# A two-layer hybrid kernel: three short products put between halves of a token unit

## The chip, the cores and the metric

The kernel runs on one core of a Trainium2 chip. The metric is the device time of one execution in microseconds (us); the median of three executions of the kernel before is 1004.25 us (999.66, 1004.25 and 1004.96). A fourth execution, the one that was profiled, took 1006.0 us. The five engines are called by the profile's names: PE (TensorE's matmuls), PEld (its weight loads), DVE (VectorE), ACT (ScalarE), POOL (GpSimd) and SP (SyncE, which here only issues DMAs).

## The reference, cut to what matters

256 tokens of width 1024 go through two layers. Each layer is a mixer, a residual with layernorm, a routed feed-forward stage with 16 experts, and again a residual with layernorm.

```python
for layer in range(2):
    mix = _mixer_ab(h, ...) if layer == 0 else _mixer_cd(h, ...)
    h = _layernorm(ALPHA * h + mix, ...)
    ffn = _moe(h, w_router, b_router, ...)
    h = _layernorm(ALPHA * h + ffn, ...)

# _mixer_ab: proj = h @ w_in; 4 retention heads (from q, k, v, gate rg) and 4 mLSTM heads (q, k, v, gate mo, mi, mf)
#   retention: scores = (q k^T) * decay;  y = scores @ v;  head norm;  * silu(rg)
#   mLSTM:     qk = (q k^T) * exp(d - m); num = qk @ v; den = qk.sum(-1); h = num / max(|den|, ..) * sigmoid(mo); norm
# _mixer_cd: 4 gated (GLA) heads and 16 SSD heads
#   GLA:       scores = q k^T weighted by exp of summed log_alpha; y = scores @ v; head norm; * silu(gr)
# _moe: probs = softmax(h @ w_router); 2 of 16 experts a token; y = sum of weighted (silu(h Wg) * (h Wu)) Wd
```

All is float32. The whole sequence is worked in two token tiles of 128 in place of the reference's chunks of 64.

## The kernel before, in words

**Units.** Weights stream in units of 2 MB (1024 x 512 of an input projection, 512 x 1024 of an output projection or of an expert) into `ring`, a buffer of six slots. SP issues the loads in program order, and waits before each for the matmul that read the slot's last unit (`freed`, waited for in `stream` and `stream_two`, L565). The mixer of layer 0 has units ab0 to ab11, that of layer 1 cd0 to cd11; each is followed by four output units (`weights_out`) and 48 expert units, six to a pair of experts.

**How a unit is multiplied.** `feature_unit` leaves features on the partitions (moving `hT`, 256 tokens wide). `token_unit` leaves tokens on the partitions: for each token tile t, it runs 8 matmuls over k, with `hT` as weights and a 512-wide moving unit, into one PSUM bank, so a unit has two halves, t = 0 and t = 1, in the two banks of a pair. Both call `mm` (L698); one such float32 matmul is two records in the trace, so a half of a token unit is 16 records. The unit's slot is free for the next load when the second half has ended. `token_unit` can be told which halves (`ts`) and which k (`ks`) to do; it claims its bank at k = 0 and signals at k = 7.

**PSUM.** There are eight banks. A table `plan`, filled by `job`, `single_job` and `pair_job` in the order of the program, says which bank a product uses and how often the bank was used before. `pair_job` takes the pairs (0, 1) and (2, 3) in turns; `single_job` takes the first bank of the next pair in the same turns; `job` names its banks. `claim` lets PE wait until the engine that reads a bank's last product has read it (`stored`), and `wait_ready` lets DVE or ACT wait for a product (`ready`).

**Order.** Each engine's order is written out by hand and is strict: an instruction that waits holds up all behind it on its engine.

- *Around the router's correction product.* PE does ab2 and ab3, then `gate_turns` (four small transposes into bank 0 and four small products into banks 2 and 3), then the product `fix`, then ab4 and ab5, then the retention scores `s_ret(0)` and `s_ret(1)`. `fix` is one product, a matrix of ones with 64 columns that DVE makes in `logit_weights` (L1907 to L1910, twice; its last instruction increments `fix_in`). DVE's order is: copy of the gate columns out of bank 0 (L1899), `logit_weights` twice, `scaled_router` (L1913), eight instructions that read the gate rows from their two banks (L1942), the copy of `fix` (L1951), then `p_ret(0)`, which waits for `s_ret(0)`. `fix` is needed by the router's correction only, after the first layer's mixer.
- *Around the fourth mLSTM head's scores.* PE does ab10, `y_ml(0)`, `y_ml(1)`, `s_ml(2)`, `s_ml(3)`, ab11, `y_ml(2)`, `y_ml(3)`, then the output units. `s_ml(hd)` is written to bank 4 for even heads and 5 for odd ones; a bank comes free when DVE's `y_ml(hd - 2)` has copied the row sums from it (L2042). DVE does all of `y_ml(0)`, then `y_ml(1)`, then `p_ml(2)` and `p_ml(3)` (the weighting of the scores, L1970), then `y_ml(2)` and `y_ml(3)`.
- *Around the fourth gated head's scores.* PE does cd4's second half, `s_gla(2)`, cd5's first half, `s_gla(3)`, `y_gla(2)`, cd5's second half, `y_gla(3)`, cd6, cd7, and then the turns of the gated heads' results (`y_turn(1, 0)`), which wait for DVE's `y_gla(3)`. `s_gla(3)` waits for `kscale`, that is for the end of DVE's `gla_head(3)` (last line L2389, eight instructions, each behind an exponential of ACT). `y_gla(hd)` needs DVE's `p_gla(hd)` (L1970). DVE's order: `gla_head(2)`, `y_gla(0)`, `y_gla(1)`, `p_gla(2)`, `gla_head(3)`, `p_gla(3)`, `y_gla(2)`, `y_gla(3)`.

Of the kernel before, what the change touches and what calls it, by code (L numbers as in the profile page):

```python
# [17 lines left out]
KC = D // P  # L18
# [84 lines left out]
def build(nc, a, out):  # L103
    with ExitStack() as ctx:
# [208 lines left out]
        def job(name, *banks):  # L313
            plan[name] = {b: uses[b] for b in banks}
            for b in banks:
                uses[b] += 1
# [4 lines left out]
        def pair_job(name):  # L321
            job(name, *((0, 1), (2, 3))[flip[0] % 2])
            flip[0] += 1

        def single_job(name):

            job(name, (0, 2)[flip[0] % 2])
            flip[0] += 1
# [41 lines left out]
            pair_job(f"ab{n}")  # L370
        single_job("gate_cols")
        pair_job("gate_rows")
        single_job("fix")
        for n in (4, 5):
            pair_job(f"ab{n}")
        for hd in range(2):
# [63 lines left out]
        def first_of(name):  # L440
            return min(plan[name])
# [4 lines left out]
        def wait_stored(eng, name, b):  # L446
            eng.wait_ge(stored[b], plan[name][b] + 1)

        def unit_no(layer, n):
            return layer * (LAYER_UNITS + MOE_UNITS) + n  # L450
# [240 lines left out]
        def _(pe):  # L691
            def claim(name, b):

                if plan[name][b]:
                    pe.wait_ge(stored[b], plan[name][b])

            def mm(o, l, r, start=True, stop=True):
                return nc.tensor.matmul(o, l, r, start=start, stop=stop)  # L698
# [21 lines left out]
            def unit_in(n):  # L720
                pe.wait_ge(ring_full[n % RING], landed(n))

            def rest_in(n):
                pe.wait_ge(ring_rest[n % RING], landed(n))
# [18 lines left out]
            def token_unit(name, n, ts=range(TB), ks=range(KC)):  # L743

                unit_in(n)
                w = ring[:, n % RING, :].rearrange("p (k n) -> p k n", k=KC)
                for t in ts:
                    b = list(plan[name])[t]
                    for k in ks:
                        if k == 0:  # L750
                            claim(name, b)
                        if t == 0 and k == KC // 2:
                            rest_in(n)
                        last = mm(bank[b][:, :], hT[:, k, t * P:(t + 1) * P], w[:, k, :], k == 0, k == KC - 1)
                        if k == KC - 1:
                            last.then_inc(ready[b], 1)
# [41 lines left out]
            def values(name, b, n_prob, v, start_cols=0, width=DV, n_heads=1, den=None, tell=True, slots=None):  # L798

                for t in range(TB):  # L800
                    for j in range(t + 1):
                        lhs = slots[:, t * P:(t + 1) * P] if j == 0 else slots[:, SEQ:SEQ + P]
                        last = mm(bank[b][:, t * DV + start_cols:t * DV + start_cols + width], lhs, v(j),
                                  j == 0, j == t)
                return last

            def score_group(b, kk, qq, parts, start=True, stop=True):
                for j in range(2):
                    last = mm(bank[b][:, j * SEQ:j * SEQ + SEQ - j * P], kk[parts, j * P:(j + 1) * P],
                              qq[parts, j * P:SEQ], start, stop)  # L810
                return last
# [48 lines left out]
            def gate_turns():  # L860
                b0 = first_of("gate_cols")
                claim("gate_cols", b0)
                pe.wait_ge(gate_ok, 1)
                for q, row in enumerate((2, 4)):
                    for t in range(TB):
                        last = nc.tensor.transpose(bank[b0][:, (q * TB + t) * 16:(q * TB + t) * 16 + HEADS],
                                                   gate_row[0:HEADS, row, t * P:(t + 1) * P],
                                                   consts[0:HEADS, C_ID:C_ID + HEADS])
                last.then_inc(ready[b0], 1)
                for q, b in enumerate(plan["gate_rows"]):  # L870
                    claim("gate_rows", b)
                    for hd in (2 * q, 2 * q + 1):

                        last = mm(bank[b][:, (hd % 2) * SEQ:(hd % 2 + 1) * SEQ],
                                  consts[0:HEADS, C_ID + hd:C_ID + hd + 1].to_broadcast([HEADS, P]),
                                  gate_row[0:HEADS, 3, :])
                    last.then_inc(ready[b], 1)

            gate_turns()
            b0 = first_of("fix")  # L880
            claim("fix", b0)
            pe.wait_ge(fix_in, 1)
            mm(bank[b0][:, 0:4 * EXPERTS], all_ones, route[:, 4:6, :, :].rearrange("p a t e -> p (a t e)")) \
                .then_inc(ready[b0], 1)
            for u in (4, 5):
                token_unit(f"ab{u}", unit_no(0, u))

            def s_ret(hd):
                b = first_of(f"s_ret{hd}")
# [21 lines left out]
            def s_ml(hd):  # L911
                b = first_of(f"s_ml{hd}")
                claim(f"s_ml{hd}", b)
                if hd == 0:
                    for u in (6, 7):
                        for bb in plan[f"ab{u}"]:
                            wait_stored(pe, f"ab{u}", bb)
                score_group(b, feat[:, 12 + hd, :], feat[:, 8 + hd, :], full).then_inc(ready[b], 1)

            def y_ml(hd):  # L920
                b, bd = first_of(f"y_ml{hd}"), first_of(f"s_ml{hd}")
                claim(f"y_ml{hd}", b)
                pe.wait_ge(prob_ready, hd + 1)
                if hd == 0:
                    for u in (8, 9):
                        for bb in plan[f"ab{u}"]:
                            wait_stored(pe, f"ab{u}", bb)
                slots = prob[:, hd % 2, :]

                for t in range(TB):  # L930
                    for j in range(t + 1):
                        mm(bank[bd][:, 400 + t:401 + t],
                           slots[:, t * P:(t + 1) * P] if j == 0 else slots[:, SEQ:SEQ + P], ones_col[:, :],
                           j == 0, j == t)
                values("", b, 0, lambda j: tok[:, 2, j, hd * DV:(hd + 1) * DV], slots=slots) \
                    .then_inc(ready[b], 1)
# [18 lines left out]
            y_ml(0)  # L955
            y_ml(1)
            s_ml(2)
            s_ml(3)
            token_unit("ab11", unit_no(0, 11))
            y_ml(2)  # L960
            y_ml(3)

# [387 lines left out]
            def s_gla(hd):  # L1350
                b = first_of(f"s_gla{hd}")
                claim(f"s_gla{hd}", b)
                pe.wait_ge(kscale, hd + 1)
                mm(bank[b][:, P:SEQ], k_far[:, hd % 2, :], dec[:, hd, SEQ:])
                for i in range(SEQ // GLA_BLOCK):
                    j, c = i // 4, i * GLA_BLOCK
                    last = mm(bank[b][:, j * P + c:j * P + c + GLA_BLOCK], k_blocks[:, i, :],
                              feat[:, hd, c:c + GLA_BLOCK])
                last.then_inc(ready[b], 1)

            def y_gla(hd):
                b = first_of(f"y_gla{hd}")
                claim(f"y_gla{hd}", b)
                wait_stored(pe, f"s_gla{hd}", first_of(f"s_gla{hd}"))
                if hd == 0:
                    for u in (2, 3):
                        for bb in plan[f"cd{u}"]:
                            wait_stored(pe, f"cd{u}", bb)
                values("", b, 0, lambda j: tok[:, 0, j, hd * DV:(hd + 1) * DV],
                       slots=prob[:, hd % 2, :]).then_inc(ready[b], 1)  # L1370
# [8 lines left out]
            token_unit("cd4", unit_no(1, 4), (1,))  # L1379
            s_gla(2)  # L1380
            token_unit("cd5", unit_no(1, 5), (0,))
            s_gla(3)
            y_gla(2)
            token_unit("cd5", unit_no(1, 5), (1,))
            y_gla(3)
            feature_unit("cd6", unit_no(1, 6), plain)
            feature_unit("cd7", unit_no(1, 7), plain)
# [1167 lines left out]
```

## Time and profile before

| | |
|---|---|
| three executions, median | 1004.25 us |
| the profiled execution | 1006.0 us, span of its instructions 1004.2 us |
| PE busy | 964.2 us (96% of the span), 3984 records |
| PEld busy | 514.2 us (51%) |
| DVE busy / ACT busy / POOL busy | 298.6 / 223.9 / 15.3 us |
| mean granted clock of TensorE | 0.990 of full speed |
| moved by DMA | 278.86 MB, mean 278 GB/s |
| longest chain | PE 79%, DMA 15%, DVE 3%, issue 1%, ACT 1% |

A stretch is given as from:to in us from the start of the span. "PEclk" is the share of the full clock that TensorE was granted in it: 1.00 is 2.4 GHz and 0.50 is 1.2 GHz. In a timeline, the bracket behind a row is the idle time of that engine just ahead of it and who ended it. Busy time on PE is modelled, so an end can lie some hundredths of a microsecond after the next start; the distance from one start to another is the safer measure.

### The profile page before, as it was taken

The numbers are of one execution on the slowest core, as the hardware profiler recorded it, in microseconds if no ns is written. First come the engines' busy times: TensorE is split into PE (matmuls) and PEld (weight loads), VectorE is DVE, ScalarE is ACT, GpSimd is POOL, SyncE is SP. The second block draws the span as 40 slices with busy tenths as digits, with TensorE's granted clock in tenths as the row PEclk, the third lists the DMA queues.
The fourth block names the chain that finished last, engine by engine and source line by source line (L and its number), as shares of the span: only waits on it lengthen the run. The fifth ranks groups of instructions, "written<-read, shape, count | busy, mean of one in ns | idle before, by whom it ended". The sixth has DMA issues, their size and how long they took to land.

```text
span 1004.2 us, 10005 instructions
## 1 busy us (share of the span) xinstructions
PE 964.2 (96%) x3984; PEld 514.2 (51%) x3984; DVE 298.6 (30%) x773; ACT 223.9 (22%) x466; POOL 15.3 (2%) x29
## 2 busy tenths in 40 slices
PE   8989999999999999989999999999999999999986
PEld 7644775554543355333385557888445433443322
DVE  4230162321431212120335433564316111131203
ACT  1120243211121112110202433431532121111101
POOL 2000000000000000000000000000000000000001
PEclk9999999999999999999999989999999999999999
DMA  8982334153789999999994423352655899999993
GB/s 275 333 317 88 134 118 149 61 210 125 270 342 404 422 422 412 397 420 421 396 388 157 156 85 118 134 210 79 241 224 211 324 399 421 420 422 420 419 418 148
DMA packets 65780, 278.86 MB, mean 278 GB/s; under 512 B 8852, under 2 KB 9216, under 8 KB 41920
## 3 DMA queue, kind: packets, MB, share of 16 engines
q1 hardware_dynamic: 63856, 271.60, 69.0%
q0 software_dynamic: 1872, 6.53, 1.9%
q8 instruction: 37, 0.61, 0.2%
q14 instruction: 15, 0.12, 0.0%
HBM read 277.04 MB, written 1.06 MB: 277 GB/s over the span
## 4 chain that ended last, share of the span: by engine, by line
PE 79%; DMA 15%; DVE 3%; issue 1%; ACT 1%; SPq 0%; DVEq 0%
PE bank L698 75%; DMA ring<-in_moe_w_up 14%; PE bank L1068 1%; DMA ring<-in_w_in_ab 1%; PE bank L1429 1%; PE bank L1073 1%; PE bank L794 1%; PE bank L975 0%; ACT feat L1497 0%; PE bank L1016 0%; DVE stat L2279 0%; ACT rstd L1497 0%; DVE hT L2286 0%; DVE h L2521 0%; DVE yT L2389 0%
## 5 line engine op out<-in xcount | busy, mean ns | idle before, releaser
L698 PE MATMUL bank<-ring,hT 128*64 128x512 f32 (+1 forms) x800 | 277.1, 604 | 11.6 <-DMA ring<-in_moe_w_up 5.4
L698 PE MATMUL bank<-ring,feat 128*64 128x512 f32 (+1 forms) x1152 | 228.5, 595 | 2.9 <-ACT feat L1497 2.7
L698 PEld LDWEIGHTS bank<-ring,hT 128*64 128x64 f32 (+1 forms) x800 | 108.5, 165 | 161.0 <-issue 153.3
L698 PE MATMUL bank<-hT,ring 128*128 128x256 f32 x768 | 168.4, 380 | 1.3 <-DMA ring<-in_w_in_ab 1.1
L698 PEld LDWEIGHTS bank<-hT,ring 128*128 128x128 f32 x768 | 145.8, 191 | 21.4 <-DMA ring<-in_w_in_ab 1.9
L1497 ACT ACTIVATE feat<-bank 32x512 f32<-32x512 f32 (+3 forms) x128 | 60.9, 494 | 388.2 <-PE bank L698 244.6
L698 PEld LDWEIGHTS bank<-ring,feat 128*64 128x64 f32 (+1 forms) x1152 | 74.1, 131 | 142.5 <-issue 131.1
L698 PE MATMUL bank<-ring,yT 128*128 128x512 f32 x256 | 112.8, 595 | 0.0
L2269 DVE COPY feat<-bank 32x512 f32<-32x512 f32 (+1 forms) x56 | 38.5, 687 | 145.7 <-PE bank L698 145.2
L698 PEld LDWEIGHTS bank<-ring,yT 128*128 128x128 f32 x256 | 47.8, 190 | 55.5 <-issue 54.6
L2259 DVE TENSOR_TENSOR feat<-feat,bank 128x512 f32<-128x512 f32 x16 | 11.0, 688 | 175.8 <-PE bank L698 175.8
L1497 ACT ACTIVATE tok<-bank 128x512 f32<-128x512 f32 x28 | 16.3, 593 | 124.7 <-PE bank L698 124.7
L698 PE MATMUL bank<-tok,h 128*128 128x256 f32 x128 | 37.7, 429 | 0.9 <-DVE tok L2146 0.9
L698 PEld LDWEIGHTS bank<-tok,h 128*128 128x128 f32 x128 | 32.5, 331 | 11.4 <-issue 11.1
L1497 ACT ACT_TABLE_LOAD x26 | 33.4, 1283 | 2.1 <-PE bank L698 1.7
L1068 PE MATMUL bank<-feat 128*128 128x512 f32 x64 | 30.9, 607 | 1.0 <-ACT feat L1497 1.0
L2009 DVE SCALAR_TENSOR_TENSOR feat<-bank,cols_cd,feat 128x255 f32<-128x255 f32 (+2 forms) x48 | 23.1, 481 | 25.7 <-ACT feat L1497 24.6
L1497 ACT ACTIVATE feat<-feat 128x256 f32<-128x256 f32 (+1 forms) x40 | 16.9, 445 | 35.8 <-DVE feat L2009 35.7
L1497 ACT ACTIVATE rstd<-mv,eps 128x2 f32<-128x2 f32 (+1 forms) x20 | 5.9, 295 | 75.2 <-DVE mv L2085 42.5
L698 PE MATMUL bank<-tok,hT 128*64 128x512 f32 x48 | 21.3, 592 | 0.0
L1520 ACT ACT_TABLE_LOAD x16 | 20.5, 1283 | 0.3
L1068 PEld LDWEIGHTS bank<-feat 128*128 128x128 f32 x64 | 10.9, 191 | 16.8 <-issue 12.5
(251 smaller groups left out, 568.7 us busy)
## 6 DMA issues: line engine op xcount, KB each, us to landing
ring<-in_moe_w_up SPq DMA_DIRECT2D x60, 1024.0 KB, 17.1
ring<-in_moe_w_gate SPq DMA_DIRECT2D x56, 1024.0 KB, 14.2
ring<-in_moe_w_down SPq DMA_DIRECT2D x56, 1024.0 KB, 12.1
ring<-in_w_in_ab SPq DMA_DIRECT2D x24, 1024.0 KB, 9.1
ring<-in_w_in_cd SPq DMA_DIRECT2D x24, 1024.0 KB, 13.5
ring<-in_w_out_ab SPq DMA_DIRECT2D x8, 1024.0 KB, 5.9
ring<-in_moe_w_down SPq DMA_DIRECT2D x16, 512.0 KB, 17.3
ring<-in_w_out_cd SPq DMA_DIRECT2D x8, 1024.0 KB, 6.0
```

The lines of the kernel that those rows point to most:

```text
L698: return nc.tensor.matmul(o, l, r, start=start, stop=stop)
L794: last = nc.tensor.transpose(bank[b][:, k * SEQ + t * P:k * SEQ + (t + 1) * P], src[:, t, c * P:(c + 1) * P], ident)
L1068: return nc.tensor.matmul(bank[4 + 2 * t + q][:, :], selw_t[:, t, :], ye[:, t, q * 512:(q + 1) * 512], start=start, stop=False, skip_group ...
L1073: last = nc.tensor.transpose(bank[0][:, c * P:(c + 1) * P], hid[:, c:FF:FF // P], ident)
L1429: last = nc.tensor.matmul(bank[b][e * SSD_HD:(e + 1) * SSD_HD, c * SEQ + j * P:(c + 1) * SEQ], xdt[:, j, hd * SSD_HD:(hd + 1) * SSD_HD], p ...
L1497: return nc.scalar.activation(o, i, f, **kw)
L1520: act.preload_act_table_set("natural_log_exp_and_others")
L2009: ins = V.scalar_tensor_tensor(out=o, in0=bank[b][:, (m % 2) * SEQ:(m % 2 + 1) * SEQ - back], scalar=cols[:, c:c + 1], in1=o, op0=ALU.mult ...
L2259: V.tensor_tensor(hid, sil, bank[3][:, :], ALU.mult) \
L2269: ins = V.tensor_copy(ye[r, t, 512:1024], bank[3][r, :])
```

## The change

`fix` moves from the turns of the pairs to bank 5 and from ahead of ab4 to between ab4's halves. `s_ml(3)` moves from ahead of ab11 to between its halves. `y_gla(2)` now comes right after cd5's first half, and `s_gla(3)` comes after the first four of the eight k of cd5's second half. Since `fix` takes no turn any more, all later `pair_job`s have the other pair: ab4 has banks 0 and 1 (it had 2 and 3), ab5 has 2 and 3, and so on through both layers up to cd11, which has 2 and 3 (it had 0 and 1). The orders of DVE, ACT, POOL and SP in the program are unchanged.

```diff
@@ -370,7 +370,7 @@
         single_job("gate_cols")
         pair_job("gate_rows")
-        single_job("fix")
+        job("fix", 5)
         for n in (4, 5):
             pair_job(f"ab{n}")
@@ -877,13 +877,14 @@
             gate_turns()
+            token_unit("ab4", unit_no(0, 4), (0,))
             b0 = first_of("fix")
             claim("fix", b0)
             pe.wait_ge(fix_in, 1)
             mm(bank[b0][:, 0:4 * EXPERTS], all_ones, route[:, 4:6, :, :].rearrange("p a t e -> p (a t e)")) \
                 .then_inc(ready[b0], 1)
-            for u in (4, 5):
-                token_unit(f"ab{u}", unit_no(0, u))
+            token_unit("ab4", unit_no(0, 4), (1,))
+            token_unit("ab5", unit_no(0, 5))
@@ -955,8 +956,9 @@
             s_ml(2)
+            token_unit("ab11", unit_no(0, 11), (0,))
             s_ml(3)
-            token_unit("ab11", unit_no(0, 11))
+            token_unit("ab11", unit_no(0, 11), (1,))
             y_ml(2)
             y_ml(3)
@@ -1379,9 +1381,10 @@
             s_gla(2)
             token_unit("cd5", unit_no(1, 5), (0,))
+            y_gla(2)
+            token_unit("cd5", unit_no(1, 5), (1,), range(KC // 2))
             s_gla(3)
-            y_gla(2)
-            token_unit("cd5", unit_no(1, 5), (1,))
+            token_unit("cd5", unit_no(1, 5), (1,), range(KC // 2, KC))
             y_gla(3)
```

## Rows read from the trace of the kernel before

**Rows 1.** Busy time by stretch (engines, PEclk, DMA share, GB/s): the two expert stages.

```profile
290.00:494.00 204.00, 196.38 (x915) 76.78 (x912) 36.16 (x91) 29.59 (x61) 0.00 (x0) 0.99 1.00 413
...
785.00:990.00 205.00, 195.81 (x908) 75.13 (x911) 36.13 (x92) 27.90 (x58) 1.05 (x2) 1.00 0.98 405
```

**Rows 2.** Waits of SP's DMA queue: total us, times, longest.

```profile
SPq L565 <- PE bank L698: 434.1, 74, 23.5
```

**Rows 3.** Waits of PE: total us, times, longest.

```profile
PE bank L698 <- DMA ring<-in_moe_w_up: 5.9, 10, 1.4
PE bank L698 <- issue: 3.8, 2, 2.1
...
PE bank L698 <- DVE yT L2389: 2.2, 1, 2.2
PE bank L698 <- DVE rec L2042: 1.9, 1, 1.9
...
PE bank L698 <- DVE route L1910: 1.4, 1, 1.4
...
PE bank L698 <- DVE feat L1942: 1.1, 1, 1.1
```

**Rows 4.** Timeline of PE: gate rows, `fix`, ab4 with ab5; then ab8 with ab9.

```profile
68.76 1.97 PE L698 MATMUL bank<-spare,consts 4*128 4x256 f32 x8
72.16 0.41 PE L698 MATMUL bank<-route,consts 128*128 128x64 f32 x2 [1.43 <-DVE route L1910]
73.67 30.75 PE L698 MATMUL bank<-ring,hT 128*128 128x512 f32 x64 [1.10 <-DVE feat L1942]
...
142.40 27.63 PE L698 MATMUL bank<-ring,hT 128*128 128x512 f32 x64
```

**Rows 5.** Timeline of DVE beside it: gate columns' copy, gate rows' readers.

```profile
68.93 0.18 DVE L1899 COPY gate_col<-bank 128x16 f32<-128x16 f32 x1 [14.50 <-PE bank L866]
...
72.13 2.69 DVE L1942 SCALAR_TENSOR_TENSOR feat<-bank,gate_col,consts 128x256 f32<-128x256 f32 x8
```

**Rows 6.** Busy time and clock by 2 us, in ab4's first half.

```profile
74.00:76.00 2.00, 2.00 (x3) 0.80 (x3) 0.95 (x4) 0.00 (x0) 0.00 (x0) 0.50 0.85 313
```

**Rows 7.** Timeline of PE: `s_ml(2)`, `s_ml(3)`, ab11.

```profile
190.59 0.82 PE L698 MATMUL bank<-feat 128*128 128x256 f32 x4
193.27 0.92 PE L698 MATMUL bank<-feat 128*128 128x256 f32 x4 [1.86 <-DVE rec L2042]
194.03 13.90 PE L698 MATMUL bank<-ring,hT 128*128 128x512 f32 x32
```

**Rows 8.** Timeline of PE: cd4's second half to cd7.

```profile
576.87 7.03 PE L698 MATMUL bank<-ring,hT 128*128 128x512 f32 x16
...
583.74 0.38 PE L698 MATMUL bank<-yT 128*128 128x128 f32 x2
...
585.66 7.11 PE L698 MATMUL bank<-ring,hT 128*128 128x512 f32 x16
595.03 0.60 PE L698 MATMUL bank<-yT 128*128 128x128 f32 x2 [2.25 <-DVE yT L2389]
...
608.59 1.46 PE L698 MATMUL bank<-tok,spare 128*128 128x256 f32 x6
609.88 27.79 PE L698 MATMUL bank<-hT,ring 128*128 128x256 f32 x128
```

**Rows 9.** Timeline of DVE beside it: `p_gla(2)`, end of `gla_head(3)`, last of `y_gla(3)`.

```profile
590.31 0.55 DVE L1970 SCALAR_TENSOR_TENSOR spare<-bank,consts 128x384 f32<-128x384 f32 x1
...
592.92 1.96 DVE L2389 SCALAR_TENSOR_TENSOR yT<-yT,feat 128x128 f32<-128x128 f32 x8
...
614.36 0.88 DVE L2416 SCALAR_TENSOR_TENSOR tok<-bank,rstd,tok 128x256 f32<-128x256 f32 x2 [0.60 <-ACT rstd L1497]
```

**Rows 10.** Busy time and clock by stretch: `s_gla(3)`; then 440:450.

```profile
596.00:600.00 4.00, 4.00 (x17) 3.82 (x17) 0.56 (x1) 0.46 (x1) 0.00 (x0) 0.50 0.02 4
...
440.00:450.00 10.00, 9.03 (x35) 3.53 (x37) 3.39 (x11) 0.21 (x1) 0.00 (x0) 0.83 1.01 419
```

## The prediction

> **What bounds the kernel now.** I read the page first: PE is busy 96% of the span and is 79% of the chain that ended last. So any time in which PE stands idle, or runs at the lower clock, outside a stage that something else sets, is time of the kernel. I then asked for busy time by stretch, to find stages with another limit. The two expert stages are such: the DMA engines are busy for 1.00 and 0.98 of them at 413 and 405 GB/s, with PE busy for 196.38 of 204 us and 195.81 of 205 [rows 1]. Everything that the change touches lies in the mixers, ahead of these stages.
>
> The third question is whether time won ahead of an expert stage is kept behind it. The waits of SP's queue answer it: in the expert loads SP stood 434.1 us, in 74 waits, for a matmul to free a slot [rows 2]. The loads do not run by a clock of their own. They start when PE has finished with the slots, so an earlier PE makes them start earlier, and the same number of bytes then ends earlier by as much.
>
> The fourth view is the list of PE's waits. Four rows in it belong to the change: 1.4 us for DVE's `logit_weights` (L1910), 1.1 for the gate rows' readers (L1942), 1.9 for the row sums of `y_ml(1)` (L2042) and 2.2 for `gla_head(3)` (L2389) [rows 3]. They sum to 6.6 us. The last view is the timeline around each with the granted clock, and it shows a second cost: behind two of the three places PE runs at clock 0.50, which is 1.2 GHz [rows 6, 10].
>
> **The change part by part.** I take each place from a start ahead of it to one behind it, and rebuild the same list of work at the pace that the trace has for it undisturbed.
>
> *`fix` between ab4's halves.* Now: the gate rows end at 68.76 + 1.97 = 70.73; PE waits 1.43 us, runs `fix` in 0.41, waits 1.10, and ab4 with ab5 end at 73.67 + 30.75 = 104.42. That is 33.69 us [rows 4]. The two units took 30.75 us where ab8 with ab9, the same 64 records, took 27.63 [rows 4]; the 3.12 us between them are the lower clock, 0.50 in 74:76 [rows 6]. After: ab4's first half can start at 70.73. Its bank is now 0, which DVE had emptied at 68.93 + 0.18 = 69.11 [rows 5]. A half lasts 27.63 / 4 = 6.9 us, so `fix` comes up at 77.6; its input was there by 72.16, when it ran before [rows 4]. Bank 5 was last used by the gate products, long read. ab5 now has banks 2 and 3, which hold the gate rows until 72.13 + 2.69 = 74.82 [rows 5], and it claims them at about 85. New stretch: 27.63 + 0.41 = 28.04. Gain 33.69 - 28.04 = 5.65 us, of it 2.53 idle and 3.12 clock. On DVE the copy of `fix` now waits until 78; behind it stands `p_ret(0)`, which waits for a score product that PE makes after ab5, at 98.8, so nobody feels it. Bank 5 goes next to `s_ret(1)`, 20 us later. The idle time is hidden by ab4's first half; if bank 0 were not free, the wait would be back at the same place.
>
> *`s_ml(3)` between ab11's halves.* Now, from the start of `s_ml(2)` to that of ab11: 194.03 - 190.59 = 3.44 us, with a wait of 1.86 us in it. One undisturbed score product is 194.03 - 193.27 = 0.76, two are 1.52 [rows 7]. Gain 1.92 us. Here the idle time brought no lower clock: ab11's 32 records took 13.90 us [rows 7], and half of ab8 with ab9 is 13.8 [rows 4]. After, `s_ml(3)` comes up at 191.35 + 6.9 = 198.3 on the old scale; its bank was read by 193.27, when it ran before [rows 7]. Nobody is late next: DVE's `p_ml(3)` follows in half a us and `y_ml(2)` and `y_ml(3)` stand behind another 6.9 us half. ACT's work on ab11's first half comes earlier, not later.
>
> *`y_gla(2)` ahead, `s_gla(3)` between the quarters.* Now, from the start of cd5's first half to that of cd6: 609.88 - 585.66 = 24.22 us [rows 8]. Undisturbed prices: a half of a token unit 583.74 - 576.87 = 6.87, a gated head's scores 585.66 - 583.74 = 1.92, a head's values 609.88 - 608.59 = 1.29 [rows 8]. The list is two halves, one score product and two values: 13.74 + 1.92 + 2.58 = 18.24. Gain 5.98 us, of it 2.25 idle [rows 8] and 3.73 clock (0.50 in 596:600 [rows 10]). Covers, on the old scale: `y_gla(2)` comes up at 585.66 + 6.87 = 592.5, and its weighted scores are there at 590.31 + 0.55 = 590.9 [rows 9], 1.6 us earlier. The quarter behind it runs 593.8 to 597.3; `gla_head(3)` ends at 592.92 + 1.96 = 594.9 [rows 9], 2.4 us ahead of `s_gla(3)`. `s_gla(3)` ends at 599.2, DVE's `p_gla(3)` at about 599.9, and PE comes to `y_gla(3)` at 602.6, so 2.7 us are left there. Were a cover gone, PE would wait its shortfall and no more. DVE's `y_gla(3)` ended at 614.36 + 0.88 = 615.2 [rows 9], and the turns that need it start behind 27.79 us of cd6 and cd7, at 637.5 [rows 8]; both ends move together.
>
> *What the trace does not show: a break inside a stream of equal matmuls.* Each of the three places gets one more of them. Below, it costs nothing: the start-to-start prices above already hold one change of operands each. Above, I take the 0.41 us of the lone `fix` [rows 4], counted once more at each place: 1.2 us. I take 0.2 for all three, near the lower end, since the score products, the nearest rows, are priced with their own changes in them.
>
> *The other pairs of banks.* Every later product has the other pair, and each pair is still used in turns, so a claim looks back as far as before. I count nothing.
>
> *No instruction, byte or DMA is added or removed.* SP's queue sees the same order, since a slot is freed by the second half, which comes earlier.
>
> Sum: 5.65 + 1.92 + 5.98 - 0.2 = 13.35 us. Against the profiled execution's own 1006.0 us (a span of 1004.2 and 1.8 around it) that is 992.65. That execution was 1.75 us above the median of the runs shown, so on the median's scale it is 1004.25 - 13.35 = 990.9.
>
> Of the 13.35 us, 6.85 are clock. The rows show it twice at 0.50 behind idle time of 1.1 to 2.25 us, and once at full clock behind 1.86 us. So idle time does not always bring the lower clock, and in another execution of the same kernel it may not have done so here. The Trainium skill ("TensorE: Matmul & The Clock Gate", Part 1) says the same from another side: the point at which the clock changes moves from run to run of one kernel. By that rule the clock's part might be missing in a median run, and only the idle part would be certain; by the rows of this trace the whole sum counts. That result is the first rival.
>
> **The rivals.**
>
> *The median run of before does not hold both losses of clock.* Then only idle time is won: 2.53 + 1.92 + 2.25 - 0.2 = 6.5 us, 997.75. For it: the three runs spread over 5.3 us, which is more than one loss (3.12 or 3.73), and the third place shows no loss. Against it: two of the three runs and the profiled one lie close together at the upper end, where one would expect those that hold both losses. Half-way (one loss gone) is 994.
>
> *The expert stages take the time back.* If the weight loads of a stage began at a time that PE does not set, what is won in the first mixer (7.6 us) or in the second (6.0) would turn into waits on DMA. All back would be 1004.3, the first mixer's alone 998.5. For it: DMA share 1.00 in these stages, and ten waits for `moe_w_up` that sum to 5.9 us [rows 1, 3]. Against it: SP's 434.1 us for slots [rows 2].
>
> *The change does not do what it says.* A cover that I put at 1.6 to 2.7 us may not hold, and PE then waits at the new place: at most the old 2.25 us and its clock at the gated head, so 6.0 us less gain, 996.9.
>
> *Slower.* The clock is lost elsewhere. Idle time of a us or more stays in other places: two "issue" waits, the longer 2.1 us, and ten for `moe_w_up` of up to 1.4 [rows 3]; 440:450, behind the longer one, had clock 0.83 [rows 10]. If these stretches meet the clock at another moment, each may cost 3.12 to 3.73 us. It takes four more losses (13.7 us at a mean of 3.4) to eat the gain, and six give 1004.25 - 13.35 + 20.5 = 1011. Against it: in the expert stages a slow PE partly hides behind DMA.
>
> **How the numbers follow.** The forecast (990.9, whole gain) has 0.72. The clock rival has 0.14, the expert stages 0.06, the failed cover 0.06, slower 0.02. The forecast's own range is 988 to 994: the bound of the breaks puts 1.0 us on top, one loss of clock less or more in the median run some 3 us on either side. The range that should hold 8 of 10 is 987 to 996.5: below, the fastest run shown (999.66) less 13.35 is 986.3; above, it takes in one loss of clock less in before and half of the failed cover. A measurement of this kernel can tell about 0.5%, which is 5 us, so faster is below 999.2: the forecast, nearly all of the clock rival, the failed cover and a third of the expert case make 0.93. Within 5 us of before lies 0.05, and slower than 1009.3 has 0.02.
>
> **What would show it.** In the profile after, PE's waits should have no row for L1910, L1942, L2042 or L2389 of more than 0.2 us. ab4 with ab5 and `fix` should take 28 us from the end of the gate rows, the way from cd5's start to cd6's 18.3 to 18.8 us, and the clock should be 1.00 in both. `s_ret(0)` should start 5.5 us earlier, the first output unit 7.5, the first expert 7.5, cd6 about 13.3, and the last expert as much. If the expert stages begin 7.5 us earlier and end less than that earlier, the second rival is right; if the places are mended and a new stretch at 0.50 stands elsewhere, the clock is the cause.

## The result and the profile after

| | before | after |
|---|---|---|
| median of five executions | 1004.25 us (999.66 to 1005.25) | 992.68 us (990.76 to 994.57) |
| ratio | | 0.9891, 95% interval 0.9873 to 0.9909 |
| the profiled execution, its span | 1006.0, 1004.2 us | 992.68, 990.7 us |
| PE busy / mean granted clock | 964.2 us (96%) / 0.990 | 957.7 us (97%) / 0.996 |

The change made the kernel 11.6 us faster by the medians (10.9 by the ratio, with an interval of 9.1 to 12.8). 13.35 us and 990.9 were forecast: 992.68 lies in the range given, but the forecast gain itself is just outside the interval.

PE's waits come first, in the form of [rows 3]: total us, times, longest.

```profile
PE bank L698 <- DMA ring<-in_moe_w_up: 6.3, 9, 1.4
PE bank L698 <- issue: 3.6, 2, 2.0
...
PE bank L698 <- DVE w_logit L1829: 1.6, 1, 1.6
```

All four rows that the change was aimed at are gone; the waits for weights and the two marked "issue" (the profile shows nothing that PE waited for) stand nearly as before. The timeline of PE at the first place answers to [rows 4]:

```profile
69.03 1.97 PE L698 MATMUL bank<-spare,consts 4*128 4x256 f32 x8
70.93 8.83 PE L698 MATMUL bank<-ring,hT 128*128 128x512 f32 x16
79.59 0.33 PE L698 MATMUL bank<-route,consts 128*128 128x64 f32 x2
79.76 20.82 PE L698 MATMUL bank<-ring,hT 128*128 128x512 f32 x48
100.51 2.54 PE L698 MATMUL bank<-feat 64*128 64x256 f32 x16
```

There is no idle time left, and the last three halves take 20.82 us, the full pace. But ab4's first half takes 8.83 us where 6.9 were priced. The clock by 2 us in that half (columns as in [rows 6]) shows where the time went:

```profile
72.00:74.00 2.00, 2.00 (x4) 0.76 (x3) 2.00 (x7) 0.00 (x0) 0.00 (x0) 0.54 1.05 409
74.00:76.00 2.00, 2.00 (x4) 0.87 (x3) 1.08 (x4) 0.00 (x0) 0.00 (x0) 0.60 1.01 381
```

PE is busy for all of both stretches, and for all of 70:72 ahead of them, and is still granted near half the clock (1.2 GHz most of the time). From the start of the gate rows to that of `s_ret(0)` it is 100.51 - 69.03 = 31.48 us now and 104.34 - 68.76 = 35.58 before: 4.1 us less, not 5.65. The rest of the forecast for this place, the covers, holds.

The second place, in the form of [rows 7], and the first score sums behind it:

```profile
186.76 0.82 PE L698 MATMUL bank<-feat 128*128 128x256 f32 x4
187.41 7.03 PE L698 MATMUL bank<-ring,hT 128*128 128x512 f32 x16
194.28 0.82 PE L698 MATMUL bank<-feat 128*128 128x256 f32 x4
194.93 7.03 PE L698 MATMUL bank<-ring,hT 128*128 128x512 f32 x16
201.80 0.72 PE L698 MATMUL bank<-ones_col,spare 128*128 128x1 f32 x6
```

From `s_ml(2)` to the sums it is 15.04 us, and was 207.76 - 190.59 = 17.17: 2.13 less (1.92 forecast). A score product costs 0.65 us from start to start where PE did not stand before it. The third place, in the form of [rows 8]:

```profile
578.44 7.11 PE L698 MATMUL bank<-ring,hT 128*128 128x512 f32 x16
585.39 1.46 PE L698 MATMUL bank<-tok,spare 128*128 128x256 f32 x6
586.69 3.60 PE L698 MATMUL bank<-ring,hT 128*128 128x512 f32 x8
590.12 0.38 PE L698 MATMUL bank<-yT 128*128 128x128 f32 x2
590.34 1.87 PE L698 MATMUL bank<-feat,yT 128*128 128x32 f32 x16
592.05 3.68 PE L698 MATMUL bank<-ring,hT 128*128 128x512 f32 x8
595.56 1.46 PE L698 MATMUL bank<-tok,spare 128*128 128x256 f32 x6
596.86 27.79 PE L698 MATMUL bank<-hT,ring 128*128 128x256 f32 x128
```

This is 596.86 - 578.44 = 18.42 us, against 24.22: 5.80 less (5.98 forecast). The quarter does its work: DVE's last instruction for `kscale`, in the form of [rows 9], and then `p_gla(3)`:

```profile
585.70 1.96 DVE L2392 SCALAR_TENSOR_TENSOR yT<-yT,feat 128x128 f32<-128x128 f32 x8
592.32 0.56 DVE L1973 SCALAR_TENSOR_TENSOR spare<-bank,consts 128x384 f32<-128x384 f32 x1 [4.66 <-PE bank L698]
```

It ends at 587.66, 2.5 us ahead of `s_gla(3)` at 590.12, and the weighted scores are there at 592.88, 2.7 us ahead of `y_gla(3)`. I had put these at 2.4 and 2.7.

The expert stages, moved by what was won ahead of them and in the form of [rows 1], and SP's wait for slots, in the form of [rows 2]:

```profile
284.00:488.00 204.00, 195.84 (x918) 76.62 (x915) 37.28 (x92) 30.34 (x61) 0.00 (x0) 1.00 1.01 414
772.00:977.00 205.00, 196.15 (x912) 74.94 (x915) 36.16 (x92) 27.87 (x58) 1.05 (x2) 1.00 0.98 405
```

```profile
SPq L565 <- PE bank L698: 430.5, 74, 23.1
```

The first expert starts at 276.87 and not 282.82, cd0 at 495.98 and not 503.20: 5.95 us were won at the entry of the stage and 7.22 at its end. The stage took nothing back. The extra 1.27 us are no work of the change: from the first expert to cd0 the thirteen profiles of this document (of before, after and eleven experiments) take 218.8 to 221.1 us, with and without the edits. Nor do they go with the clock. The kernel before had 0.83 in 440:450 [rows 10] and took 220.4 us, this one had 1.00 and took 219.1; but the third experiment below had 1.00 and took 220.3, and the first had 0.68 in 438:442 and took 219.2. So the low clock does not show in the length of this stage, in which DMA is busy throughout. The clock of the first experiment in 438:442, then of the third in 440:450:

```profile
438.00:442.00 4.00, 3.48 (x12) 1.32 (x14) 2.61 (x10) 0.00 (x0) 0.00 (x0) 0.68 1.01 418
...
440.00:450.00 10.00, 9.04 (x43) 3.69 (x45) 3.29 (x11) 0.60 (x1) 0.00 (x0) 1.00 1.01 416
```

So the two profiled executions are 13.3 us apart, which is the forecast's sum, but not by its terms, so that agreement is luck: 4.1 + 2.1 + 5.8 at the three places, and 1.3 from a stage that the change does not touch. The medians, 11.6 us apart, are the better guide, and the question is why they are below 13.35.

Of the signs that I named, the waits are gone and cd6 starts 13.0 us earlier, as forecast. Three came out short: `s_ret(0)` starts 3.8 us earlier and not 5.5, the first output unit 6.0 and the first expert 6.0 and not 7.5. What they miss, 1.5 to 1.7 us, is about the 1.7 us lost in ab4's first half.

### The profile page after: what moved, and what is told of

It is laid out like the page before. It is cut to its first block, busy times and chain, and to the rows that moved or that the text cites. A ratio compares the mean times of both kernels' runs of the same rounds, so it can differ in the third digit from the quotient of the medians.

```text
span 990.7 us, 10007 instructions
## 1 busy us (share of the span) xinstructions
PE 957.7 (97%) x3984; PEld 511.4 (52%) x3984; DVE 298.8 (30%) x773; ACT 223.8 (23%) x466; POOL 15.3 (2%) x29
## 4 chain that ended last, share of the span: by engine, by line
PE 83%; DMA 13%; DVE 2%; issue 1%; ACT 1%; SPq 0%; DVEq 0%
PE bank L698 78%; DMA ring<-in_moe_w_up 12%; PE bank L1070 1%; DMA ring<-in_w_in_ab 1%; PE bank L1075 1%; PE bank L1432 1%; PE bank L794 1%; ACT feat L1500 0%; PE bank L977 0%; PE bank L1018 0%; DVE stat L2282 0%; DVE hT L2289 0%; DVE feat L2262 0%; DVE h L2524 0%; PE bank L1401 0%
## 5 line engine op out<-in xcount | busy, mean ns | idle before, releaser
L698 PE MATMUL bank<-ring,hT 128*64 128x512 f32 (+1 forms) x800 | 274.1, 597 | 10.7 <-DMA ring<-in_moe_w_up 5.7
L698 PEld LDWEIGHTS bank<-tok,h 128*128 128x128 f32 x128 | 32.5, 331 | 11.4 <-issue 11.1
L1070 PEld LDWEIGHTS bank<-feat 128*128 128x128 f32 x64 | 10.9, 191 | 16.8 <-issue 12.5
```

Of the source, the lines that this page charges most:

```text
L1070: return nc.tensor.matmul(bank[4 + 2 * t + q][:, :], selw_t[:, t, :], ye[:, t, q * 512:(q + 1) * 512], start=start, stop=False, skip_group ...
```

## The experiments

All ratios are to the kernel before, run on the same chip in between the experiment's runs. Times in the text are medians; a gain in us is worked out from the ratio, which rests on all runs and can differ from the distance of the medians by a us or more. A timeline or a clock is that of one profiled execution.

**Each edit alone.** The first three experiments are the parts of the change. The first is the diff's first two hunks (bank 5, `fix` between ab4's halves):

```diff
-        single_job("fix")
+        job("fix", 5)
...
+            token_unit("ab4", unit_no(0, 4), (0,))
             b0 = first_of("fix")
...
-            for u in (4, 5):
-                token_unit(f"ab{u}", unit_no(0, u))
+            token_unit("ab4", unit_no(0, 4), (1,))
+            token_unit("ab5", unit_no(0, 5))
```

> Only the first of the three moves: the correction product in bank 5 and between ab4's halves (with it all later pairs of banks change). If idle time and the clock lost behind it both count: ab4 with ab5 end 5.65 us earlier than in the kernel before, or 4.1 us if the first half of ab4 again runs in part at 0.50, as it did in the changed kernel's profile (8.83 us instead of 7.0). The whole kernel gains the same, 1000.1 to 998.6. If median runs hold no loss of clock: 2.5 us, 1001.7. If the expert stage takes it back: cd6 starts where it did, 1004.3.

Measured: 999.93 us against 1004.06, ratio 0.9962 (0.9948 to 0.9975), so 3.8 us. The profile (a slower execution of the twelve, 1001.94 us) has the same slow first half as the changed kernel's, and a slow ab11 behind the wait that it still has. First ab4, then ab11 (timeline of PE):

```profile
70.76 8.83 PE L698 MATMUL bank<-ring,hT 128*128 128x512 f32 x16
...
189.27 0.92 PE L698 MATMUL bank<-feat 128*128 128x256 f32 x4 [1.86 <-DVE rec L2043]
190.03 15.60 PE L698 MATMUL bank<-ring,hT 128*128 128x512 f32 x32
```

The 15.60 us are 1.70 more than the 13.90 of [rows 7]. So this wait can bring the lower clock too; in the profile that I forecast from, it had not.

The second is the third hunk:

```diff
             s_ml(2)
+            token_unit("ab11", unit_no(0, 11), (0,))
             s_ml(3)
-            token_unit("ab11", unit_no(0, 11))
+            token_unit("ab11", unit_no(0, 11), (1,))
```

> Only the fourth mLSTM head's scores between ab11's halves. My term: 1.92 us, all idle, no clock in it; 1002.3. By the profile of the changed kernel it is 2.1 us. If the expert stage takes time back: first output unit 1.9 us earlier, cd0 where it was, 1004.3. Slower: ab11's first half or s_ml(3) waits, or ab11's 32 records take more than 14.7 us; 1005 or more.

Measured: 998.85 against 1004.06, ratio 0.9963 (0.9947 to 0.9978), 3.7 us, at least 2.2. That is more than my term, and the interval leaves it out. Its place itself shows 15.04 us, as in the changed kernel. The same profile has two shorter losses of clock at places that the edit does not touch: ab4 with ab5, ahead of it in the program, take 29.38 us (30.75 before), and the way from cd5 to cd6 is 603.32 - 580.73 = 22.59 us (24.22 before). So part of what this execution gained did not come from the edit.

```profile
73.33 29.38 PE L698 MATMUL bank<-ring,hT 128*128 128x512 f32 x64 [1.10 <-DVE feat L1943]
```

The third is the last hunk:

```diff
-            s_gla(3)
             y_gla(2)
-            token_unit("cd5", unit_no(1, 5), (1,))
+            token_unit("cd5", unit_no(1, 5), (1,), range(KC // 2))
+            s_gla(3)
+            token_unit("cd5", unit_no(1, 5), (1,), range(KC // 2, KC))
```

> Only the gated heads' edit. From the start of cd5's first half to that of cd6: 18.2 to 18.5 us instead of 24.22, so 5.8 to 6.0 us less, and 998.3 for the kernel, if both idle time and clock count. If only the idle 2.25 us counts in a median run: 1002.0. If the second expert stage takes it back: cd6 is 5.9 us early and the last expert is not, 1004.3.

Measured: 998.94 against 1004.06, ratio 0.9952 (0.9934 to 0.9969), 4.8 us. The way from cd5 to cd6 is 603.32 - 584.90 = 18.42 us. All three parts gain, and the product of the ratios is 0.9878, close to the whole.

**Only the bank.**

```diff
-        single_job("fix")
+        job("fix", 5)
```

> Only the plan's line: the correction product in bank 5, its place ahead of ab4 as before. The wait for its input (1.43 us) must stay. ab4 now has banks 0 and 1, so its wait of 1.10 us for the gate rows' readers should go. What the two theories on the clock say: if the clock falls because PE stood idle for 1.4 us and 1.1 us, part or all of the 3.1 us in ab4's first half may go; if it falls because of the thin products ahead (four partitions) as well, ab4's first half stays above 8.5 us. Whole kernel 1.1 us less than before at clock as before (1003.1), up to 4.2 less (1000.0). If other banks cost anything later, it shows as a start of cd6 or of the second expert stage that is later than that.

Measured: 1002.14 against 1004.06, ratio 0.9986 (0.9972 to 1.0001), which does not exclude no change. The timeline shows that the new pairs do what they should, and no more:

```profile
71.96 0.66 PE L698 MATMUL bank<-route,consts 128*128 128x64 f32 x2 [1.43 <-DVE route L1910]
72.42 30.56 PE L698 MATMUL bank<-ring,hT 128*128 128x512 f32 x64
```

The wait for the gate rows' readers is gone, the 1.43 us stay, and ab4 with ab5 take as long as in [rows 4] (30.75). The other banks cost nothing further on: cd6 starts 2.8 us earlier than before.

**Without the quarter.** The kernel before, with `y_gla(2)` first:

```diff
-            s_gla(3)
             y_gla(2)
+            s_gla(3)
             token_unit("cd5", unit_no(1, 5), (1,))
```

> The kernel before with y_gla(2) ahead of s_gla(3), and cd5's second half whole behind both. My covers: y_gla(2) takes 1.29 us of the wait of 2.25 us, so s_gla(3) still waits about 1.0 us. If the lower clock comes with long idle time, 1.0 us may be too short for it: way from cd5's start to cd6's 19.3 us, gain 5 us, 999. If any wait there brings it: 21 to 22.5 us, gain 2 to 3, 1001.5.

Measured: 1001.33 against 1004.14, ratio 0.9973 (0.9962 to 0.9984), 2.7 us. Timeline of PE:

```profile
592.42 1.46 PE L698 MATMUL bank<-tok,spare 128*128 128x256 f32 x6
594.83 0.46 PE L698 MATMUL bank<-yT 128*128 128x128 f32 x2 [0.95 <-DVE yT L2389]
595.12 1.88 PE L698 MATMUL bank<-feat,yT 128*128 128x32 f32 x16
596.83 8.81 PE L698 MATMUL bank<-ring,hT 128*128 128x512 f32 x16
```

The wait shrank to 0.95 us, as priced, and behind it the half of cd5 takes 8.81 us where 7.03 is the full pace: 1.8 us of clock are lost still. The way to cd6 is 606.77 - 585.47 = 21.30 us. The quarter is worth 21.30 - 18.42 = 2.9 us in these two profiles, three times the wait it hides, and 2.1 us by the two ratios.

**The waits filled, nothing moved.** Four kernels leave the order of the kernel before alone and give PE products of constants in place of idle time. Nobody reads their results.

```diff
+            claim("y_gla3", first_of("y_gla3"))
+            for _ in range(5):
+                mm(bank[7][:, 0:SEQ], all_ones, cmask[:, 0:SEQ])
             s_gla(3)
```

> The kernel before, with five 256-wide products of constants into the next values' bank ahead of s_gla(3): 2.1 us of PE work whose result nobody reads, in place of idle time of 2.25 us. The order and the wait's end are as before. This takes the clock's part by itself. If the lower clock comes from idle time: the way from cd5's start to cd6's falls from 24.22 to 20.5 us, and the kernel gains 3.7 us (1000.4). If it comes from the score products (32 columns wide) or from chance: no gain, 24 us or more and 1004.

Measured: 1001.09 against 1004.14, ratio 0.9970 (0.9957 to 0.9982), 3.0 us. Timeline of PE:

```profile
583.95 7.11 PE L698 MATMUL bank<-ring,hT 128*128 128x512 f32 x16
590.90 2.32 PE L698 MATMUL bank<-consts 128*128 128x256 f32 x10
593.31 0.46 PE L698 MATMUL bank<-yT 128*128 128x128 f32 x2
...
604.85 10.52 PE L698 MATMUL bank<-hT,ring 128*128 128x256 f32 x48
```

`s_gla(3)` starts no earlier behind cd5's half than before (9.36 us, and 9.37 in [rows 8]), yet cd6 follows after 20.90 us and not 24.22. These 3.3 us are the clock's part at this place, shown by itself. The score products, 32 columns wide, are not its cause, since they run here as before. (This profile is the fastest of the twelve executions, 999.35 us; the ratio's 3.0 us rest on all of them.)

```diff
             s_ml(2)
+            claim("ab11", 0)
+            for _ in range(4):
+                mm(bank[0][:, 0:SEQ], all_ones, cmask[:, 0:SEQ])
             s_ml(3)
```

> The kernel before, with four 256-wide products of constants into a free bank between s_ml(2) and s_ml(3): 1.7 us of PE work nobody reads in the place of 1.86 us idle; order and waits as before. Moving s_ml(3) alone gained 3.7 us by the ratio where my term was 1.92, all idle. If the rest was clock (the first experiment's profile has ab11 at 15.60 us for 13.90 behind this same wait): this kernel gains 1.5 to 2 us, 1002.3, and ab11 takes 13.9 us. If the move gained by something else, or by chance of the runs: 1004.1, no gain.

Measured: 1003.66 against 1004.05, ratio 0.9997 (0.9980 to 1.0013). No gain. ab11 takes 13.90 us in its profile, but so it does in most of the kernels that have this wait: of the seven profiles with it unfilled (before and six experiments), only the first experiment's shows the lower clock. The explanation in the expectation, that the 3.7 us of the edit alone hold a part of clock at this place, falls with this. What remains of them above 2.1 us stays open and may be the spread of the runs: that interval reached down to 2.2, and the edit's own profile was luckier at two other places.

```diff
             claim("fix", b0)
+            for _ in range(3):
+                mm(bank[b0][:, 0:SEQ], all_ones, cmask[:, 0:SEQ])
             pe.wait_ge(fix_in, 1)
...
+            claim("ab5", 1)
+            for _ in range(2):
+                mm(bank[1][:, 0:SEQ], all_ones, cmask[:, 0:SEQ])
```

> The kernel before, with three such products ahead of the correction product and two between it and ab4, 1.3 and 0.9 us of PE work in waits of 1.43 and 1.10 us. If idle time brings the lower clock: ab4 with ab5 take 27.7 us instead of 30.75, kernel 3 us less, 1001.1. If it is the thin products of the gate rows ahead (the changed kernel showed 8.83 us for a first half with no idle time ahead, and 7.13 in another profile): ab4 with ab5 stay between 28.5 and 30, kernel 0 to 2 us less.

Measured: 1001.76 against 1004.05, ratio 0.9975 (0.9958 to 0.9991), 2.5 us. Timeline of PE, and under it the clock in 72:74:

```profile
70.25 1.89 PE L698 MATMUL bank<-consts 128*128 128x256 f32 x6
71.93 0.53 PE L698 MATMUL bank<-route,consts 128*128 128x64 f32 x2
72.25 2.02 PE L698 MATMUL bank<-consts 128*128 128x256 f32 x4
74.07 27.98 PE L698 MATMUL bank<-ring,hT 128*128 128x512 f32 x64
```

```profile
72.00:74.00 2.00, 2.00 (x7) 1.71 (x6) 2.00 (x7) 0.00 (x0) 0.00 (x0) 0.50 1.05 407
```

The clock fell here too, with no idle time, while PE ran the fillers: the last four took 2.02 us where the same four records took 1.08 in the next kernel. But it was back sooner, and ab4 with ab5 lost 0.35 us and not 3.12.

All three fillers together:

> The kernel before with all three waits filled (the five, four and five products of the three experiments before); no product of the kernel is moved. By span less the time lost to the clock (span times 1 minus the mean granted clock, over all runs) the changed kernel won 6.0 us of idle time and 5.5 us of clock. So this kernel should win the clock's share alone: 5 to 6 us, 998.6, ratio 0.9945, and its mean granted clock should be near the changed kernel's 0.996. If the clock's share is not brought by these waits: ratio above 0.998. If it wins as much as the changed kernel, idle time was no cost, which I don't believe.

Measured: 1001.25 against 1004.05, ratio 0.9976 (0.9966 to 0.9986), 2.4 us. This is less than I expected and less than the three fillers promised singly (0.9970, 0.9997 and 0.9975 multiply to 0.9942). Its profile is clean at all three places (27.70 us for ab4 with ab5, 13.90 for ab11, 20.90 from cd5 to cd6), but it is the fastest of the twelve executions, 998.73 us and 2.5 below their median, so it cannot speak for the others. By the means of the table below the shortfall is 2.3 us (3.2 against 2.9 + 0.3 + 2.3) with a standard error of about 1.1. It can be chance; if it is not, its cause is open.

**The thin products.** The changed kernel, with the gate rows' four small products taken out of `gate_turns` into a function of their own, `gate_spread`, and put between ab4's halves:

```diff
                 last.then_inc(ready[b0], 1)
+            def gate_spread():
                 for q, b in enumerate(plan["gate_rows"]):
                     claim("gate_rows", b)
...
             gate_turns()
             token_unit("ab4", unit_no(0, 4), (0,))
+            gate_spread()
             b0 = first_of("fix")
```

> The changed kernel, with one more move: the four small products of the gate rows (four partitions) come between ab4's halves, ahead of the correction product, and not ahead of ab4; the transposes of the gate columns stay. In the changed kernel and in the first experiment ab4's first half took 8.83 us with no idle time ahead. If the thin products ahead bring the lower clock there: both halves of ab4 take 7.0 us now, and the kernel is 1.8 us faster than the changed one (991). If it is the place in time or chance: a half of ab4 or ab5 is still 8.5 us or more and the kernel is as the changed one. If a thin stretch anywhere brings it, ab4's second half takes 8.8.

Measured: 992.82 against 1004.14, ratio 0.9887 (0.9870 to 0.9903). Timeline of PE:

```profile
69.13 7.10 PE L698 MATMUL bank<-ring,hT 128*128 128x512 f32 x16 [0.36 <-DVE gate_col L1904]
76.17 1.99 PE L698 MATMUL bank<-spare,consts 4*128 4x256 f32 x8
78.08 0.43 PE L698 MATMUL bank<-route,consts 128*128 128x64 f32 x2
78.36 20.82 PE L698 MATMUL bank<-ring,hT 128*128 128x512 f32 x48
```

Both halves are at full pace, which speaks for the thin products as the cause, until one looks at the control, the changed kernel run again:

> The changed kernel once more, on the same chip and beside the same runs of the kernel before as the three others. Its ratio to before was 0.9891 (0.9873 to 0.9909); the product of the three single edits' ratios is 0.9962 x 0.9963 x 0.9952 = 0.9878. If the edits add up, 0.988 to 0.990; if they share a gain, nearer 0.992.

Measured: 993.03 against 1004.14, ratio 0.9885 (0.9866 to 0.9905), the same as the first time and the same as with the rows later. Its timeline of PE, and the clock in 72:74:

```profile
70.69 7.13 PE L698 MATMUL bank<-ring,hT 128*128 128x512 f32 x16
77.67 0.33 PE L698 MATMUL bank<-route,consts 128*128 128x64 f32 x2
77.83 20.82 PE L698 MATMUL bank<-ring,hT 128*128 128x512 f32 x48
```

```profile
72.00:74.00 2.00, 2.00 (x6) 0.95 (x5) 2.00 (x8) 0.00 (x0) 0.00 (x0) 1.00 1.05 410
```

The same program has 8.83 us for this half in one execution and 7.13 in another. So one clean profile proves nothing on the thin products, and what makes the clock fall there with PE busy is not settled. The kernel with the rows later is no faster than the changed one, and no experiment gave a version that is.

**Idle time and clock over all runs.** Each run gives a span and a mean granted clock, so span x (1 - clock) is an estimate of the time that the lower clock cost (it counts idle time at the lower clock too, and a low clock in the expert stages that costs nothing; and the clock is given to 0.001, which is 1 us, so only means over many runs count). Means, in us, against the runs of before on the same chip; n is the number of runs of the kernel named, and the standard error of an entry is 0.4 to 1.0 us. The last column is the wait taken away; a filler takes none away, PE works through it.

| kernel | n | span less | of it clock | the rest | wait taken away, by the timeline |
|---|---|---|---|---|---|
| `fix` moved | 12 | 3.5 | 2.0 | 1.5 | 2.53 |
| `s_ml(3)` moved | 12 | 3.8 | 2.2 | 1.6 | 1.86 |
| `s_gla(3)`, `y_gla(2)` moved | 6 | 4.8 | 2.4 | 2.4 | 2.25 |
| bank only | 12 | 1.5 | 0.2 | 1.3 | 1.10 |
| `y_gla(2)` first, no quarter | 12 | 2.6 | 2.3 | 0.3 | 1.30 |
| filled at the gated head | 12 | 2.9 | 2.8 | 0.1 | 0 |
| filled at the mLSTM head | 12 | 0.3 | 0.3 | 0.0 | 0 |
| filled at `fix` | 12 | 2.3 | 2.4 | 0.0 | 0 |
| all filled | 12 | 3.2 | 3.3 | -0.1 | 0 |
| changed kernel, gate rows later | 4 | 11.4 | 5.9 | 5.5 | 6.3 |
| changed kernel | 10 | 11.7 | 5.5 | 6.2 | 6.6 |

The last row is 990.45 us (clock cost 3.9) against 1002.14 (9.3, 81 runs). The column "rest" mostly behaves as it should: near zero where only fillers were added, and 6.2 us of the 6.6 that the timelines lost as idle time. One row does not fit: with `y_gla(2)` first, 1.30 us of wait went and the rest is 0.3 us, with a standard error of 0.4. So the split of one small edit is not to be relied on.

**The places over all profiles.** The other way is to take each place from every profile that keeps its waits unfilled and every one that has its edit whole. From the gate rows to `s_ret(0)` the mean is 35.12 us in six against 30.92 in three, 4.2 less (the kernel with the gate rows later is left out here, its list of work is another). From `s_ml(2)` to the sums it is 17.42 in seven against 15.04 in four, 2.4 less. From cd5 to cd6 it is 23.97 in six against 18.42 in four, 5.6 less. These 12.1 us come near to the measured 11.6 (10.9 by its ratio, and 11.5 by that of the repeated run).

## Why the prediction was right, and where its sizes were off

*PE bounds the mixers, and time won there is kept.* Right. The expert stages begin and end earlier by what was won ahead of them. The rival in which they take it back is refuted by three single edits as well: the `fix` edit enters the first stage 2.3 us earlier and reaches cd0 3.5 earlier; the mLSTM edit 3.8 and 4.9 (1.4 of the 3.8 stem from ab4 with ab5, not from the edit); the gated heads' edit comes to the second stage (779.68 before, 773.11 with it) 6.6 earlier.

*`fix` between ab4's halves: 5.65 us.* The step's idle part, 2.53, and its covers (the work put into each wait) held. The term of the clock, 3.12, was mis-sized: the two units' time is back to pace in one of three profiles with the edit, and 1.7 us stay lost in ab4's first half in the other two. The profile has 4.1 us, the edit alone 3.8 by its ratio, and the mean over profiles is 4.2. This is most of the way from 13.35 to what was measured. I took it that the lower clock goes when the idle time goes; the runs show it coming in the same stretch with PE busy throughout, less long.

*`s_ml(3)` between ab11's halves: 1.92 us.* Right by the timeline (2.13); the 0.2 us more are two score products at 0.65 us, which I had priced at 0.76 from the one right behind the wait. The edit alone measured 3.7 with a lower bound of 2.2; the filler shows no part of the clock that would explain it.

*The gated heads: 5.98 us.* Right by the timeline in all four profiles that have the edit (18.42 us in each). Its clock term, 3.73, was that of one execution. In the six profiles that keep the full wait the way is 22.59 us in one (the mLSTM edit's) and 24.22 to 24.27 in five, and 20.90 in the two that have it filled: the clock's part is 1.7 to 3.4 us. The ratio gives the edit 4.8 us, the mean over profiles 5.6.

*The breaks: 0.2 us for three.* Right, as far as such small terms can be read. In the repeated run the gate rows' way to `s_ret(0)` has 27.89 us from ab4's start where 27.63 and `fix` were priced at 28.04, and the two quarters with the scores between take 593.34 - 584.46 = 8.88, against 6.87 + 1.92 = 8.79.

*The other pairs: nothing.* Right; they take away the wait of 1.10 us and change no other.

*The rivals.* That the change does not do what it says is refuted: no cover failed. The rival "no loss of clock in the median run of before" (6.5 us) is refuted: the gain is 9.1 us at least, all seven profiles that keep both waits at `fix` or the first of them lose clock in ab4 with ab5 (29.38 to 30.78 us against 27.63), all six that keep the full wait at the gated head lose it there, and the fillers at these two places change no wait and no order and still win 2.5 and 3.0 us. Its half-way form (one loss gone, 994) is not excluded by the ratio alone; what came out is in between. I gave the clock 6.85 us, its size in one execution; over the runs it is 5.5. The profiles show why: the kernels with the waits mostly lose less than the 3.12 us of that execution in ab4 with ab5, and the changed kernel still lost 1.7 there in one of its two. Together with 6.2 for idle time that makes the 11.7. These traces agree with the rule that I cited beside it (the Trainium skill, "TensorE: Matmul & The Clock Gate", Part 1): the point of the change of clock moves from run to run of one kernel, as the same half of 7.13 and 8.83 us shows.

## What to carry to other kernels

A short wait on the engine that bounds a kernel can cost more than its length. Here 6.6 us of waits of 1.1 to 2.25 us cost 11.7 us, since the clock fell behind most of them (a wait of 0.95 us, too, was followed by 1.8 us lost). It was not so at each: behind the 1.86 us at the mLSTM head the clock fell in one profile of seven. So hide such a wait behind work that is ready, cut finely enough to cover all of it: a half of a unit, or a quarter. The two tightest covers of the quarter had 2.5 and 2.7 us to spare; tighter ones were not tried. Take the clock's part from means over runs, not from one profile, and check how far a place moves among profiles of one kernel before you explain a difference by the change.

## What the runs showed of the hardware that I had not expected

The granted clock was 0.54 and 0.60 in stretches where PE was busy throughout, with no idle time ahead (72:76 of the changed kernel), and 1.00 in 72:74 of the same program in another execution. A lower clock did not show in the length of a stage in which DMA was busy throughout (219.2 us with 0.68 in 438:442, 220.3 without such a stretch). Filling three waits with products of constants won 2.4 us by the ratio, though singly the fillers won 3.0, 0.3 and 2.5; I know no reason for it, and chance is not excluded.
